# One gate pass and one value pass per expert, with the output blocks one by one between the next expert's input blocks

## The chip, the cores and the metric

The kernel runs on one core of one Trainium2 chip. The metric is the device time of one execution in microseconds. A core has a matrix engine (PE, with its weight loads on a row of its own, PEld), a vector engine (DVE), a scalar engine (ACT), a fourth compute engine (POOL) and a queue engine (SP) that issues nearly all transfers; 16 DMA engines carry those out.

## The reference, cut to what matters

Two layers over 256 tokens, in fp32. The first is Fourier and windowed attention with a dense SwiGLU, the second is differential attention with a SwiGLU of 8 experts, of which each token takes two. The change touches only the experts:

```python
def moe_swiglu(h, router_w, w_in, w_out):
    logits = jnp.einsum('btd,de->bte', h, router_w)
    top_vals, top_idx = lax.top_k(logits, TOP_K)             # TOP_K = 2
    gates = jax.nn.softmax(top_vals, axis=-1)
    ...
    for e in range(N_EXPERTS):                               # 8
        out = out + combine[..., e:e + 1] * swiglu(h, w_in[e], w_out[e])

def swiglu(h, w_in, w_out):                                  # 1024 -> 2 x 3584 -> 1024
    g, u = jnp.split(h @ w_in, 2, axis=-1)
    return (jax.nn.silu(g) * u) @ w_out
```

The weights of one expert are 1024 x 7168 and 3584 x 1024 numbers of 4 bytes, 44.04 MB; all eight are 352.3 MB.

## The kernel before

Each expert works on at most 96 gathered tokens (a "large" place) or 64 (a "small" one). The places 0, 2, 4, 6 are large, 1, 3, 5, 7 are small, and the last expert is so a small one. In words, for one expert: a gather (matrix products with a one-hot table) brings its tokens into PSUM, ACT writes them as `h_te` (L1047); the input passes multiply them with the gate and the value columns of `expert_in_w`; ACT takes silu of the gate sums (L1066), DVE multiplies by the value sums (L2290), PE turns the product round in 128x128 tiles (`transposes`, L1654), ACT copies the turned tiles to `work` (L1072); the output blocks multiply them with `expert_out_w` into PSUM; ACT and DVE split the result into two parts `y_split` (L1078, L2263), PE spreads it back to token order (`combine`, with `onehot_t`), and DVE adds it to `y_acc` (L2276).

The hidden width of 3584 is cut in two halves, A with 2048 columns and B with 1536. So an expert has four input passes (GA, UA, GB, UB) of 8 blocks each, one block for each 128 rows of the input: 128 partitions with rows of 8 KB (A) or 6 KB (B). Its output has 14 blocks of 256 rows, 1 MiB each, 8 for A and 6 for B. In all an expert has 46 blocks. The order in which PE uses them is one list, which also is the order of the transfers:

```python
LAST = in_pass("GB") + out_blocks("A", 0, 4) + in_pass("UB") + out_blocks("A", 4, 8)
CYCLE = LAST + in_pass("GA", 1) + out_blocks("B", 0, 3) + in_pass("UA", 1) + out_blocks("B", 3, 6)
LAST = LAST + out_blocks("B", 0, 6)
```

The passes GA and UA in a cycle are those of the next expert. The blocks land in 18 slots of 8 KB a partition, taken in turn (`RING0`); a B block fills three quarters of its slot. PE counts every block that it has used in the semaphore `used`, and SP fetches block n when block n - 18 has been used:

```python
sp.wait_ge(used, B_MOE + n - RING0 + 1)
fetch(0, min((n - len(HEAD)) // EB, NE - 1), n, order)
```

So SP's issues are in the order of use, and each slot is refilled as soon as PE is through with it. The first 18 blocks are fetched while the attention of the second layer still runs, as the places of its weights and buffers come free (the waits on `lo_done`, `scores`, `pv_done`, `used`, `hn_done` in SP's `experts`). Rounds 1 and 2 of `experts` serve tokens above the capacity, behind a branch on `overflow`; in the profiled execution they are not entered.

Of the kernel before, what the change touches and what calls it, by code (L numbers as in the profile page):

```python
# [41 lines left out]
HALVES = ("A", "B")  # L42
WIDTH = {"A": 2048, "B": 1536}
OUTS = {"A": 8, "B": 6}
ROUNDS = 3
RING0 = 18
RING = 14
# [22 lines left out]
def in_pass(what, ahead=0):  # L70
    return [("in", what, k, ahead) for k in range(DK)]


def out_blocks(half, m0, m1):
    return [("out", half, m, 0) for m in range(m0, m1)]


HEAD = in_pass("GA") + in_pass("UA")
LAST = in_pass("GB") + out_blocks("A", 0, 4) + in_pass("UB") + out_blocks("A", 4, 8)
CYCLE = LAST + in_pass("GA", 1) + out_blocks("B", 0, 3) + in_pass("UA", 1) + out_blocks("B", 3, 6)  # L80
LAST = LAST + out_blocks("B", 0, 6)
AFTER = {"GB": 8, "UB": 20, "GA": 32, "UA": 43}
EB = len(CYCLE)
ROUND = HEAD + CYCLE * (NE - 1) + LAST
assert len(ROUND) == NE * EB
assert GROUP * 3 == CAP
# [8 lines left out]
def act_columns(cap, half):  # L95

    return {CAP: 3, SMALL: 2}[cap] * WIDTH[half] // 4
# [7 lines left out]
PIECES = {CAP: [[(0, 96, 3, 0, 512, 0, 0)],  # L105
                [(96, 32, 3, 0, 512, 0, 512), (0, 32, 4, 0, 256, 32, 512), (32, 32, 4, 0, 256, 32, 768),
                 (64, 32, 4, 0, 256, 64, 512), (96, 32, 4, 0, 256, 64, 768)]],
          SMALL: [[(0, 64, 3, 0, 512, 0, 0)], [(64, 64, 3, 0, 512, 0, 512)]]}
# [57 lines left out]
def backbone(nc, x, c, ctx_in, c_ctx, ada_w, ada_b, norm_g, mix_in_w, mix_out_w, win_sink, diff_qkv_w,  # L166
# [9 lines left out]
    WRAW = sb("w_raw", [P, RAW, BLK])  # L176
# [54 lines left out]
    _, POST2 = area(("pad_p", [P, W0 - 4096], F32), ("post2", [P, 4, D], F32))


    (WMOE, HTE, YS, PTR, YACC, ONEHOT) = area(
        ("w_moe", [P, 2 * SPL, BLK], F32), ("h_te", [P, DK, CAP], F32), ("y_split", [P, 2, D], F32R),
        ("onehot_t", [P, 2 * P], F32R), ("y_acc", [P, XT, D], F32), ("onehot", [P, XT, CAP], F32))
    _, XW = area(("pad_x", [P, W0 - BLK], F32), ("w_extra", [P, BLK], F32))
    _, HN = area(("pad_b", [P, W0 + 12288], F32), ("h_nat", [P, XT, D], F32))
    TM = RES[:, 2, 0:400]
    SIL = RES[:, 2:4, :].rearrange("p a b -> p (a b)")[:, 512:2048]  # L240

# [47 lines left out]
    ACTT = work(10240, 2048)  # L289
    SPARE = work(6144, 2, BLK)  # L290
    FREED, QFREED = work(0, 2, BLK), work(4096, BLK)
# [19 lines left out]
    w_landed = [sem(f"w_landed{i}") for i in range(RING0)]  # L311
# [101 lines left out]
    hte_first = sem("hte_first")  # L413
# [14 lines left out]
    tr_ready = sem("tr_ready")  # L428
    actt_ready = sem("actt_ready")
# [6 lines left out]
    silu_half = sem("silu_half")  # L436
    act_half = sem("act_half")
# [61 lines left out]
    LATER = [0, 1] + list(range(5, 5 + RAW + 2 * SPL))  # L499
    early = (B_DOUT + 1) % SPL  # L500
    SPLIT_SLOTS = [early, SPL + early] + [j for j in range(2 * SPL) if j % SPL != early]
    assert len(LATER) == RING

    PLACE = [3, 4, 0, 1, 2] + list(range(5, RING0))

    def turn(n):

        i = (n - len(HEAD)) % EB
        return (i % RING, 4 if i < EB % RING else RING + EB % RING if i < RING else RING) if i < EB - EB % RING else \
            (i - EB + EB % RING, RING)  # L510

    def slot_of(rnd, n):
        return LATER[turn(n)[0]] if rnd else PLACE[n % RING0]

    def ring(r):

        if r < 5:
            return SPARE[:, r, :] if r < 2 else QFREED[:] if r == 2 else FREED[:, r - 3, :]
        if r < 5 + RAW:
            return WRAW[:, (N_RAW + r - 5) % RAW, :]  # L520
        return WMOE[:, SPLIT_SLOTS[r - 5 - RAW], :] if r < RING0 - 1 else XW[:]

    def moe_landed(rnd, e, n):

        slot = slot_of(rnd, n)
        if rnd == 0:
            return 16 * (n // RING0 + 1)
        first = 16 * sum(slot_of(0, m) == slot for m in range(len(ROUND)))
        fills = [m for m in range(len(ROUND)) if slot_of(rnd, m) == slot]
        each = 16 * sum(len(HEAD) <= m < len(HEAD) + EB for m in fills)  # L530
        return first + (rnd - 1) * 16 * len(fills) + e * each + 16 * sum(m <= n for m in fills)

    def moe_view(rnd, n):

        kind, what = ROUND[n][:2]
        w = ring(slot_of(rnd, n))
        return w.rearrange("p (j n) -> p j n", j=2) if kind == "out" else w[:, 0:WIDTH[what[1]]]

# [1869 lines left out]
```

## Time and profile before

| what | value |
|---|---|
| device time, median of 3 runs | 1671.93 us (1671.19 to 1673.8) |
| the profiled execution | 1671.87 us, of which the span is 1670.0 us |
| PE busy in the span | 95% |
| DVE, ACT busy | 31%, 23% |
| moved by DMA in the span | 474.42 MB, mean 284 GB/s |
| granted PE clock | 0.986 of full speed |

The span is what the trace shows; 1.87 us of the profiled execution's time lie outside it. The expert stage begins at about 828 us of the span and takes the second half. A busy PE is not a PE at its peak, since waits inside a run of matmuls count as busy when their records overlap.

### The profile page before, as it was taken

How to read it: one execution, taken by the hardware profiler on the slowest of the kernel's cores; microseconds unless marked ns; L12 is line 12 of the kernel's file. 1: busy time of each engine (PE TensorE's matmuls, PEld its weight loads, DVE VectorE, ACT ScalarE, POOL GpSimd, SP SyncE). 2: the span in 40 equal slices, each digit the busy share in tenths (PEclk: the TensorE clock that was granted, in tenths of full speed). 3: DMA queues.
4: the chain of work that ended last, by engine and by line, in shares of the span. 5: the costliest groups of instructions: out<-in, count | busy, mean ns of one | idle time of the engine just before them, and what ended most of it. 6: DMA issues, size and time to landing. Idle time of an engine off the chain costs nothing.

```text
span 1670.0 us, 28575 instructions
## 1 busy us (share of the span) xinstructions
PE 1583.0 (95%) x12596; PEld 953.8 (57%) x12596; DVE 519.8 (31%) x791; ACT 391.1 (23%) x655; POOL 34.5 (2%) x70
## 2 busy tenths in 40 slices
PE   5999989999999989998899999999999998999986
PEld 2855678878788877866536333463435533345232
DVE  3427467665533276357500010100101001010012
ACT  3327342221232243248400111000100001100011
POOL 1000100010000000000000000000000000000000
PEclk9999999999999999999899999999999999999998
DMA  9661816676523323213699999999999999999995
GB/s 368 210 226 36 258 51 202 199 256 231 217 85 120 117 82 126 101 51 138 253 318 390 417 418 421 417 419 418 418 421 418 419 418 418 420 418 419 418 418 213
DMA packets 106754, 474.42 MB, mean 284 GB/s; under 512 B 11176, under 2 KB 35144, under 8 KB 70784
## 3 DMA queue, kind: packets, MB, share of 16 engines
q1 hardware_dynamic: 103552, 467.64, 72.0%
q0 software_dynamic: 3072, 4.88, 1.1%
q8 instruction: 101, 1.65, 0.4%
q14 instruction: 29, 0.24, 0.0%
HBM read 471.36 MB, written 1.13 MB: 283 GB/s over the span
## 4 chain that ended last, share of the span: by engine, by line
PE 64%; SPq 19%; DMA 9%; DVE 5%; issue 2%; ACT 1%; DVEq 0%; ACTq 0%
PE ps L1140 62%; SPq L601 13%; SPq L598 6%; DMA w_moe<-in_expert_out_w_dram 2%; DMA work<-in_expert_out_w_dram 2%; DMA w_raw<-in_expert_out_w_dram 2%; DMA work<-in_expert_in_w_dram 1%; DMA w_raw<-in_ada_w_dram 1%; DMA w_moe<-in_expert_in_w_dram 1%; PE ps L1323 1%; DVE work L1835 1%; PE ps L1654 1%; DVE row_max L2103 1%; DVE w_lo L1766 0%; SPq L596 0%
## 5 line engine op out<-in xcount | busy, mean ns | idle before, releaser
L1140 PE MATMUL ps<-w_hi,h_t 128*128 128x512 f32 (+1 forms) x960 | 294.6, 388 | 11.5 <-DVE h_t L1824 5.4
L1140 PE MATMUL ps<-h_t,w_hi 128*128 128x512 f32 (+1 forms) x768 | 222.5, 374 | 6.2 <-DVE h_t L1824 6.2
L1140 PEld LDWEIGHTS ps<-w_hi,h_t 128*128 128x128 f32 x960 | 180.8, 191 | 49.0 <-issue 4.1
L1766 DVE TENSOR_TENSOR w_lo<-w_raw,w_hi 128x2048 fp32r<-128x2048 f32 x57 | 130.6, 2292 | 228.3 <-ACT w_hi L738 227.9
L1140 PE MATMUL ps<-w_lo,h_t 128*128 128x512 f32 (+1 forms) x480 | 185.4, 386 | 0.0
L2290 DVE TENSOR_TENSOR residual<-residual,ps 128x1152 f32<-128x1152 f32 (+3 forms) x15 | 19.4, 1292 | 529.1 <-PE ps L1140 529.1
L738 ACT ACTIVATE w_hi<-w_raw 128x2048 fp32r<-128x2048 f32 x57 | 108.9, 1913 | 301.7 <-PE ps L1140 301.4
L1140 PE MATMUL ps<-w_moe,h_te 128*32 128x512 f32 (+2 forms) x1830 | 170.6, 520 | 5.3 <-DMA w_moe<-in_expert_in_w_dram 4.4
L1140 PE MATMUL ps<-w_raw,h_te 128*32 128x512 f32 (+2 forms) x1694 | 159.5, 519 | 7.0 <-DMA w_raw<-in_expert_in_w_dram 6.1
L1140 PEld LDWEIGHTS ps<-h_t,w_hi 128*128 128x128 f32 x768 | 141.3, 191 | 33.8 <-issue 9.2
L1140 PE MATMUL ps<-work 128*32 128x512 f32 (+6 forms) x1104 | 141.9, 498 | 11.4 <-DMA work<-in_expert_out_w_dram 5.0
L1140 PE MATMUL ps<-work,h_te 128*32 128x512 f32 (+2 forms) x1662 | 147.4, 506 | 0.9 <-ACT h_te L1047 0.5
L1140 PE MATMUL ps<-h_t,w_lo 128*128 128x512 f32 (+1 forms) x384 | 143.4, 373 | 0.0
L1140 PEld LDWEIGHTS ps<-w_moe,h_te 128*32 128x32 f32 x1830 | 67.9, 110 | 102.6 <-issue 77.6
L1140 PEld LDWEIGHTS ps<-w_raw,h_te 128*32 128x32 f32 x1694 | 61.3, 110 | 98.9 <-issue 70.2
L1140 PEld LDWEIGHTS ps<-work,h_te 128*32 128x32 f32 x1662 | 65.6, 110 | 78.8 <-issue 61.7
L1140 PEld LDWEIGHTS ps<-w_lo,h_t 128*128 128x128 f32 x480 | 91.7, 191 | 17.6
L1140 PEld LDWEIGHTS ps<-work 128*32 128x32 f32 (+3 forms) x1104 | 53.4, 128 | 79.0 <-issue 52.2
L1140 PE MATMUL ps<-w_raw,work 128*32 128x512 f32 (+1 forms) x1024 | 93.8, 513 | 3.0 <-DMA w_raw<-in_expert_out_w_dram 3.0
L1140 PEld LDWEIGHTS ps<-h_t,w_lo 128*128 128x128 f32 x384 | 73.2, 191 | 12.5
L1140 PE MATMUL ps<-w_moe,work 128*32 128x512 f32 (+1 forms) x832 | 76.2, 515 | 1.6 <-DMA w_moe<-in_expert_out_w_dram 1.6
L1140 PEld LDWEIGHTS ps<-w_raw,work 128*32 128x32 f32 x1024 | 34.3, 110 | 58.7 <-issue 42.9
(274 smaller groups left out, 1210.2 us busy)
## 6 DMA issues: line engine op xcount, KB each, us to landing
w_raw<-in_ada_w_dram SPq DMA_DIRECT2D x48, 1024.0 KB, 5.3
w_raw<-in_expert_in_w_dram SPq DMA_DIRECT2D x43, 1024.0 KB, 24.7
w_moe<-in_expert_in_w_dram SPq DMA_DIRECT2D x42, 1024.0 KB, 26.1
w_raw<-in_expert_out_w_dram SPq DMA_DIRECT2D x40, 1024.0 KB, 23.7
work<-in_expert_in_w_dram SPq DMA_DIRECT2D x37, 1024.0 KB, 23.4
w_moe<-in_expert_in_w_dram SPq DMA_DIRECT2D x45, 768.0 KB, 22.0
work<-in_expert_out_w_dram SPq DMA_DIRECT2D x33, 1024.0 KB, 23.8
w_moe<-in_expert_out_w_dram SPq DMA_DIRECT2D x33, 1024.0 KB, 23.5
```

Of the source, the lines that this page charges most:

```text
L598: sp.dma_start(w, rows.rearrange("(p j) n -> p j n", j=2)).then_inc(done, 16)
L601: sp.dma_start(w, expert_in_w[0, e, b * P:(b + 1) * P, c0:c0 + WIDTH[what[1]]]).then_inc(done, 16)
L738: act.activation(WHI[:, b % SPL, :], WRAW[:, slot_w[b], :], ACT.Copy).then_inc(hi_done, 1)
L1140: return pe.matmul(out_, l, r, start=first, stop=last, skip_group_check=True)
L1323: ins = pe.transpose(ps[:, 4 + kv, c_ * P:(c_ + 1) * P], PR0[:, 2 * (u % 2) + kv, c_ * P:(c_ + 1) * P], ID[:])
L1654: ins = pe.transpose(ps[:, 5 + x // 4, P * (x % 4):P * (x % 4) + P], src, ID[:])
L1766: dve.tensor_tensor(WLO[:, b % SPL, :], WRAW[:, slot_w[b], :], WHI[:, b % SPL, :].bitcast(F32), ALU.subtract).then_inc(lo_done, 1)
L1835: ins = dve.tensor_scalar(TF[s][:, n % 2, 256 * k:256 * k + 256], ps[:, UNIT_BANK[s][st][u], 256 * k:256 * k + 256], ACOL[:, st, 2 * u + k ...
L2103: link(dve.tensor_reduce(MX[:, p:p + 2], ps[:, p ^ 2:(p ^ 2) + 2, :], AX_X, ALU.max))
L2290: dve.tensor_tensor(SIL[:, 0:n], SIL[:, 0:n], PSF[:, 0:n], ALU.mult).then_inc(act_done, 1)
```

## The change

The halves A and B are gone. An expert now has one gate pass G and one value pass U over all 3584 columns, 8 blocks each of 128 partitions with rows of 14 KB (1.75 MiB), and 14 output blocks of 1 MiB as before, in all 30 blocks. The sums of a pass fill five PSUM banks and a quarter of a sixth (three and a half for a small place; `BANKS`), and silu, product, transposes and the copies of the turned tiles go bank by bank (`silu_bank`, `prod_bank`, `tr_bank`, `actt_bank`). The output sums lie in banks 6 and 7. The output blocks of expert e stand one by one between the input blocks of expert e + 1, from its third gate block on; those of the last expert stand alone behind its transposes.

The slots are 8 of 14 KB for input blocks and 3 of 8 KB for output blocks. A freed slot takes the next block of its own kind; only when no input blocks are left do freed input slots (but one, `KEEP`) take output blocks. SP issues in the order in which slots are freed, which is no longer the order of use.

```diff
-HALVES = ("A", "B")
-WIDTH = {"A": 2048, "B": 1536}
-RING0 = 18
...
+EB = 2 * DK + ED // 256
+BANKS = {CAP: (512,) * 5 + (128,), SMALL: (512,) * 3 + (256,)}
...
+def first_round():
+    order = [("G", 0, k) for k in range(DK)] + [("U", 0, k) for k in range(DK)]
+    for e in range(NE - 1):
+        ins = [("G", e + 1, k) for k in range(DK)] + [("U", e + 1, k) for k in range(DK)]
+        for i, b in enumerate(ins):
+            order += [b] + ([("O", e, i - 2)] if i >= 2 else [])
+    return order + [("O", NE - 1, m) for m in range(ED // 256)]
+
+IN_SLOTS, OUT_SLOTS = 8, 3
+KEEP = 4
...
+    for n, b in enumerate(USES):
+        s = place[b]
+        if s < IN_SLOTS and ins:
+            nxt = ins.pop(0)
+        elif outs and s != KEEP:
+            nxt = outs.pop(0)
+        else:
+            continue
+        place[nxt] = s
+        fetches.append((nxt, n + 1))
...
-                for n in range(RING0, len(ROUND)):
...
-                    sp.wait_ge(used, B_MOE + n - RING0 + 1)
-                    fetch(0, min((n - len(HEAD)) // EB, NE - 1), n, order)
...
+                sp.wait_ge(lo_done, B_MOE - 4)
+                fetch(0, "G", 0, 0)
+                sp.wait_ge(lo_done, B_MOE - 2)
+                fetch(0, "G", 0, 1)
+                sp.wait_ge(scores, U0 + U1)
+                fetch(0, "G", 0, 2)
+                fetch(0, "O", 0, 0)
+                sp.wait_ge(pv_done, U0 + U1)
+                fetch(0, "G", 0, 4)
+                sp.wait_ge(lo_done, B_MOE)
+                fetch(0, "G", 0, 3)
+                sp.wait_ge(used, B_MOE)
+                for k in range(5, DK):
+                    fetch(0, "G", 0, k)
+                fetch(0, "O", 0, 1)
+                sp.wait_ge(hn_done, XT)
+                fetch(0, "O", 0, 2)
...
+                for (kind, e, i), after in FETCHES:
...
+                    sp.wait_ge(used, B_MOE + after)
+                    fetch(0, kind, e, i, order)
...
+            for b, n in enumerate(BANKS[cap]):
+                if first:
+                    hold(b)
+                for q in range(4):
...
+            for e in range(NE - 1):
+                transposes(e)
+                if e:
+                    pe.wait_ge(y_lo, 2 * e)
+                gather(e + 1)
+                product("G", e + 1, 0)
+                if e:
+                    pe.wait_ge(hte_ready, DK * (e + 2))
+                    combine(e - 1, 0, 6)
+                    combine(e - 1, 1, 7)
+                product("G", e + 1, 1)
...
+            e = NE - 1
+            transposes(e)
+            pe.wait_ge(y_lo, 2 * e)
+            for m in range(ED // 256):
+                product("O", e, m)
+                if m == 1:
+                    for i in range(4):
+                        combine(e - 1, i, i)
...
+            hte(0, CAP)
+            silu(0)
+            for e in range(NE):
+                if e:
+                    yhi(e - 1)
+                transposed(e)
+                turned(e)
+                if e == NE - 1:
+                    break
+                hte(e + 1, capacity(0, e + 1))
...
+                silu(e + 1)
```

In the diff `G`, `U` and `O` name a block's kind, and the expert and the block's number follow; its last two pieces are PE's and ACT's order. SP's first issues of the stage, before the change (a row with x5 stands for five transfers; 128x2048 are rows of 8 KB, 128x1536 of 6 KB):

```order
L601 DMA w_raw<-in_expert_in_w_dram 128x2048 x4
L601 DMA work<-in_expert_in_w_dram 128x2048 x5
L601 DMA w_raw<-in_expert_in_w_dram 128x2048 x2
L601 DMA w_moe<-in_expert_in_w_dram 128x2048 x5
L601 DMA w_moe<-in_expert_in_w_dram 128x1536
L601 DMA w_extra<-in_expert_in_w_dram 128x1536
L601 DMA work<-in_expert_in_w_dram 128x1536 x5
L601 DMA w_raw<-in_expert_in_w_dram 128x1536
L598 DMA w_raw<-in_expert_out_w_dram 128x2048 x4
```

and after it:

```order
L635 DMA w_moe<-in_expert_in_w_dram 128x3584 x2
L635 DMA work<-in_expert_in_w_dram 128x3584
L632 DMA work<-in_expert_out_w_dram 128x2048
L635 DMA work<-in_expert_in_w_dram 128x3584
L635 DMA w_moe<-in_expert_in_w_dram 128x3584 x4
L632 DMA w_moe<-in_expert_out_w_dram 128x2048
L632 DMA w_extra<-in_expert_out_w_dram 128x2048
L635 DMA w_moe<-in_expert_in_w_dram 128x3584 x2
```

The first fill was 16 blocks of 1 MiB and 2 of 0.75 MiB; it is now 8 of 1.75 MiB and 3 of 1 MiB.

PE at the end of the expert stage, before the change (`w_moe,h_te` is an input block, `w_..,work` or `work` alone an output block of 8 matmuls for a small place, L1654 transposes, `y_split` a combine, `mod_rows` the spread of the last gate):

```order
L1140 MATMUL ps<-w_moe,h_te 32x512 x4
L1140 MATMUL ps<-w_moe,h_te 32x256 x4
L1140 MATMUL ps<-w_moe,work 32x512 x8
L1140 MATMUL ps<-w_extra,work 32x512 x8
L1654 MATMUL ps<-ident,residual 128x128 x6
L1140 MATMUL ps<-work 32x512 x32
L1140 MATMUL ps<-mod_rows,ident 128x128 x8
L1140 MATMUL ps<-work 32x512 x8
L1140 MATMUL ps<-w_raw,work 32x512 x24
L1140 MATMUL ps<-y_split,onehot_t 128x512 x8
```

and after it:

```order
L1663 MATMUL ps<-ident,residual 128x128 x12
L1663 MATMUL ps<-ident,w_moe 128x128 x2
L1669 MATMUL ps<-ident,onehot 64x128 x2
L1170 MATMUL ps<-w_extra,work 32x512 x8
L1170 MATMUL ps<-w_moe,work 32x512 x8
L1170 MATMUL ps<-y_split,onehot_t 128x512 x8
L1170 MATMUL ps<-w_moe,work 32x512 x8
L1170 MATMUL ps<-work 32x512 x8
L1170 MATMUL ps<-mod_rows,ident 128x128 x8
L1170 MATMUL ps<-w_moe,work 32x512 x40
L1170 MATMUL ps<-work 32x512 x8
L1170 MATMUL ps<-w_extra,work 32x512 x8
```

Behind the last transposes stood 8 output blocks (32 + 8 + 24 matmuls, 8 to a block); now all 14 stand there, and with them the combine of the expert before.

PE at the boundary between the experts 1 and 2 (a small and a large place) after the change; `onehot,h_nat` is the gather:

```order
L1663 MATMUL ps<-ident,residual 128x128 x12
L1663 MATMUL ps<-ident,w_moe 128x128 x2
L1669 MATMUL ps<-ident,onehot 64x128 x2
L1170 MATMUL ps<-onehot,h_nat 128x96 x16
L1170 MATMUL ps<-w_moe,h_te 32x512 x20
L1170 MATMUL ps<-w_moe,h_te 32x128 x4
L1170 MATMUL ps<-y_split,onehot_t 128x512 x4
```

The transposes and the gather were apart before, each with blocks on both sides; they now stand together, with no block between them.

## Rows read from the trace of the kernel before

**Rows 1.** The page: span, DMA queue, chain's engines, one transfer kind (last: issue to landing).
```profile
span 1670.0 us, 28575 instructions
...
q1 hardware_dynamic: 103552, 467.64, 72.0%
...
PE 64%; SPq 19%; DMA 9%; DVE 5%; issue 2%; ACT 1%; DVEq 0%; ACTq 0%
...
w_raw<-in_ada_w_dram SPq DMA_DIRECT2D x48, 1024.0 KB, 5.3
```

**Rows 2.** Busy time by stretch; the last three columns are clock, DMA share, GB/s.
```profile
828.00:912.00 84.00, 81.75 (x950) 40.68 (x954) 4.79 (x10) 8.50 (x15) 0.00 (x0) 1.00 0.90 330
912.00:1640.00 728.00, 708.44 (x7582) 305.03 (x7578) 60.35 (x100) 66.25 (x122) 0.00 (x0) 1.00 1.01 418
1641.00:1652.00 11.00, 10.00 (x88) 3.99 (x92) 0.00 (x0) 1.08 (x2) 0.00 (x0) 1.00 0.55 226
```

**Rows 3.** The same view of two stretches with A blocks, then three with B blocks.
```profile
1000.00:1050.00 50.00, 50.00 (x482) 18.54 (x478) 0.95 (x1) 4.95 (x10) 0.00 (x0) 1.00 1.01 420
1200.00:1250.00 50.00, 49.41 (x466) 18.31 (x462) 0.95 (x1) 4.95 (x10) 0.00 (x0) 1.00 1.01 420
...
945.00:965.00 20.00, 20.00 (x216) 6.85 (x212) 0.00 (x0) 1.02 (x1) 0.00 (x0) 1.00 1.02 418
1145.00:1165.00 20.00, 20.00 (x216) 6.89 (x212) 0.00 (x0) 0.45 (x1) 0.00 (x0) 1.00 1.01 415
...
1270.00:1290.00 20.00, 19.95 (x267) 13.98 (x263) 4.18 (x7) 2.64 (x3) 0.00 (x0) 1.00 1.01 417
```

**Rows 4.** SP's issues in order of time: start, time until the last, line, transfer, count.
```profile
691.97 34.74 SPq L601 DMA_DIRECT2D w_raw<-in_expert_in_w_dram  x4
...
818.43 0.33 SPq L601 DMA_DIRECT2D w_extra<-in_expert_in_w_dram  x1
831.32 10.63 SPq L601 DMA_DIRECT2D work<-in_expert_in_w_dram  x5
```

**Rows 5.** PE in order of time; one matmul of the program is two records.
```profile
828.48 13.08 PE L1140 MATMUL ps<-work,h_te 128*32 128x512 f32 x120 [0.52 <-ACT h_te L1047]
...
875.91 1.70 PE L1654 MATMUL ps<-ident,residual 128*128 128x128 f32 x12
877.54 9.96 PE L1140 MATMUL ps<-work,h_te 128*32 128x512 f32 x150
...
894.89 5.37 PE L1140 MATMUL ps<-w_raw,work 128*32 128x512 f32 x64
...
982.03 2.11 PE L1140 MATMUL ps<-y_split,onehot_t 96*128 96x512 f32 x8
984.07 4.08 PE L1140 MATMUL ps<-w_moe,h_te 128*32 128x512 f32 x48
...
1005.74 3.81 PE L1140 MATMUL ps<-onehot,h_nat 128*128 128x96 f32 x32
...
1011.23 5.33 PE L1140 MATMUL ps<-w_moe,work 128*32 128x512 f32 x48
...
1027.73 10.48 PE L1140 MATMUL ps<-work,h_te 128*32 128x512 f32 x96
```

**Rows 6.** ACT and DVE in order of time, after one expert's outputs.
```profile
974.43 2.76 ACT L1078 ACTIVATE y_split<-ps 96x512 fp32r<-96x512 f32 x6 [28.19 <-PE ps L1140]
...
977.22 2.42 DVE L2263 TENSOR_TENSOR y_split<-ps,y_split 32x512 fp32r<-32x512 f32 x5 [1.48 <-ACT y_split L1078]
...
1009.59 2.69 ACT L1047 ACTIVATE h_te<-ps,mod_cols,scale_cols 128x96 f32<-128x96 f32 x8 [17.26 <-PE ps L1140]
```

**Rows 7.** The end: two rows of PE in order of time.
```profile
1645.78 2.05 PE L1140 MATMUL ps<-mod_rows,ident 8*128 8x128 f32 x16
...
1657.22 2.38 PE L1140 MATMUL ps<-y_split,onehot_t 64*128 64x512 f32 x8 [1.50 <-DVE y_split L2263]
```

**Rows 8.** The last transfer in the chain that ended last (start, length, what).
```profile
1627.61 26.15 DMA w_raw<-in_expert_out_w_dram
```

More of the change, by code:

```diff
@@ L512, in slot_of @@
[L512 to L525, printed above, removed]
-        if rnd == 0:
[L527 to L537, printed above, removed]
[L539 to L543 removed]
+    def slot_view_moe(s):
+        if s < IN_SLOTS:
+            at = (8192, 0, -4096, 4096, -1, 11776, 15360, 18944)[s]
+            if s == 2:
+                return work(4096, ED)
+            return work(0, ED) if s == KEEP else WMOE[:, at:at + ED]
+        return (work(7680, BLK), WMOE[:, 22528:24576], XW[:])[s - IN_SLOTS]
@@ L1053, in silu @@
-            def silu(e, half, after):
-                J = 2 * (NE * rnd + e)
-                act.wait_ge(used, after)
-                first = rnd == 0 and isinstance(e, int) and e == 0 and half == "A"
-                if not first:
-                    act.wait_ge(tr_ready, J + HALVES.index(half))
-                if first:
-                    for b in range(3):
-                        act.activation(SIL[:, 512 * b:512 * b + 512], ps[:, b, :],
-                                       ACT.Silu).then_inc(silu_half if b < 2 else silu_done, 1)
-                    return
-                n = act_columns(capacity(rnd, e), half)
-                act.activation(SIL[:, 0:n], PSF[:, 0:n], ACT.Silu).then_inc(silu_done, 1)
@@ L1114, in _ @@
+            for h in range(2):
+                act.activation(POST[3][0][:, 0, 512 * h:512 * h + 512], ps[:, 4 + h, :], ACT.Copy).then_inc(gate_kept, 1)
+            yhi(NE - 1)
         flag = []
@@ L1610, in out_block @@
+        def out_block(m, w):
+            for j in range(2):
+                first = m == 0 and j == 0
+                last = m == 13 and j == 1
+                for tg in range(3):
+                    mm(ps[group(tg), 6, :], hidden(m, j, tg), w[:, j, 0:512], first, last)
+                mm(ps[group(3), 6, :], hidden(m, j, 0), w[:, j, 512:1024], first, last)
                 for n, (tg, c_) in enumerate(QUARTERS):
-                    ins = mm(ps[group(n), 4, 0:256], hidden(half, m, j, tg),
+                    ins = mm(ps[group(n), 7, 0:256], hidden(m, j, tg),
@@ L2343, in experts @@
-            cycle(NE - 1, True)
-            gate(n0 + NE, order[NE - 1] + 1 if rnd == 0 else NE)
-            ylo(NE - 1)
-            for i in range(4):
-                accumulate(n0 + NE, i, i)
-            dve.wait_ge(acc_done, (n0 + 9) * 4 - 3)
+                with dve.Fori(0, NE) as e:
+                    onehot(place_of(e), e)
+                    product(e)
+                    ylo(e)
+                    gate(e, e)
+                    for i in range(4):
+                        accumulate(e, i, i)
@@ L2350, in _ @@
+            e = NE - 1
+            for x, bank in ((e - 1, 0), (e, 0)):
+                ylo(x)
+                gate(x, order[x])
+                for i in range(4):
+                    accumulate(x, i, i)
+            dve.wait_ge(acc_done, 4 * NE + 1)
         flag = []
```

685 lines of the change are left out of this document (318 added, 367 removed).

## The prediction

> **What bounds the kernel now.** I read the page first, then the stretches, then SP's and PE's order of time. The page says PE 64% and DMA 9% of the chain, SP's queue 19% [rows 1]; that looks like a PE kernel, but the expert stage has to be read by stretches. From 912 to 1640 us the 16 DMA engines are busy all the time (share 1.01) and move 418 GB/s [rows 2]. PE's busy time there is nearly full as well, but it works on blocks that the transfers let it have: what ends the stage is the last weight block, which lands at 1627.61 + 26.15 = 1653.8 us [rows 8], and after it come only one output block, the split, four combines and the finish. From 1641 to 1652 the share is only 0.55 at 226 GB/s [rows 2], with the last blocks still out: about half of the engines are through at 1641 and the others run to 1653. A block has landed when its slowest engine has delivered. So the pace that counts is not 418 but what lands: of 352.3 MB, 18.35 MB are the first fill (16 blocks of 1.049 MB, 2 of 0.786) and 84 x 0.330 = 27.7 MB come until 912 [rows 2, 4]; the other 306.2 MB take until 1653.8, 741.8 us, or 412.8 GB/s.
>
> Before 912 the transfers are not the bound. SP's first refill is at 831.32, after PE's first block from 828.48 on [rows 4, 5], and until 912 only 330 GB/s are moved [rows 2], since PE frees slots of 1 MiB that are refilled with 0.75 MiB blocks.
>
> **Step 1, the opening.** The first fill is 17 MiB in place of 17.5, and its places come free at the same events (691.97 to 818.43) [rows 4]. Large input blocks cost 13.08 / 5 = 2.62 (A) and 9.96 / 5 = 1.99 us (B) [rows 5]; the new block has the same matmul columns in both, 4.6 us. 16 of them: 828.5 + 73.6 = 902.1. Each frees 1.75 MiB and takes 1.75 MiB, 399 GB/s, so that at 902 all of 24 input and 3 output blocks are issued, 47.2 MB. Then PE frees nothing: 20 transposes at 1.70 / 12 = 0.14 us, 2 for the one-hot table, a gather of 3.81, and the first small input block, 10.48 / 6 + 4.08 / 3 = 3.1 us [rows 5]. The next slot is free at about 912.5, the next byte moves at 913.5, and the DMA engines stand idle for some 6 us. Yet at 913.5 47.2 MB are there, against 46.1 + 0.6 = 46.7 MB now: 1.2 us **gained**, no more.
>
> **Step 2, the rate of longer rows.** A block pair of 256 rows (8 and 6 KB) becomes one of 128 rows of 14 KB. Over the stage this takes 8 x 16 x 128 = 16384 of the 103552 packets away [rows 1]. Stretches in which only 8 KB rows move show 420 GB/s, stretches in which six tenths of the bytes come in 6 KB rows 418, 415 and 417 [rows 3]. With 16 engines that is 0.03810 and 0.03840 ns a byte for an engine; the difference over 0.6 x (1/6144 - 1/8192) gives 12.4 ns fixed cost a packet. An input block saves 8 packets an engine, 0.099 us; for the 104 input blocks after the opening 10.3 us **gained**. Bounds: nothing, if the differences in these rows are noise (the rows differ among themselves as much), and 15.6 us with 415 against 420. I take 10.3, the mean, for it rests on more than one row of each kind. The Trainium skill (DMA: Bandwidth & Descriptors, Why small descriptors are slow) puts the fixed cost of a packet at about 3 cycles and 32 bytes, and says that joining descriptors pays only at 256 bytes and below. By it the gain would be an estimated 4.7 ns a packet, 4 us in all, and the time some 6 us more than my sum.
>
> **Step 3, does PE keep up in the middle?** The same columns as before, so the blocks cost the same: large output 5.37 / 2, small output 5.33 / 3 [rows 5], with some 0.2 us of a run's last record taken off 2.65 and 1.74. New is that transposes and gather stand together behind the last output block of the expert before, whose sums have to leave banks 6 and 7 first: for a large one ACT's copies take 2.76 us [rows 6], DVE's subtractions end at 979.6, 2.4 us after ACT's 977.2 [rows 6], then come gather 3.81 and the first `h_te` (2.69 / 8) [rows 5, 6]: 9.5 us without a block, and 7.3 us where the transposes hide a small one's split. The combine costs 2.11 as before. A large input phase is 16 x 4.6 + 14 x 1.74 + 9.5 + 2.1 = 109.6 us, a small one 16 x 3.05 + 14 x 2.65 + 7.3 + 2.1 = 95.3; a pair 204.9. The transfers of a pair take 88.08 MB / 412.8 = 213.4, less 32 x 0.099 = 210.2. So PE keeps up, by 5 us a pair. Silu and product bank by bank cost nothing where PE's next bank covers them: ACT's six pieces of a split take 2.76 us [rows 6], some 0.5 us each, against 2.62 / 3 = 0.87 us of a bank on PE [rows 5]; without that cover it would be about 1 us an expert.
>
> But the order of issue matters. An output block is fetched when the one three before it has been used, behind the input blocks issued ahead, which are needed only eight input blocks later. PE thus waits for output blocks while its input blocks land some 30 us early, and the queue holds three pairs at most, 8.65 MB or 21 us (26 us now [rows 8]). Of these 2.8 us are latency (5.3 us from issue to landing without a queue [rows 1], of which 2.5 are the moving of 1 MiB) and 5.7 us PE's own pair; a gap of 9.5 us leaves some 3 us. I allow 0.6 us of idle DMA at three boundaries, 1.8 us **lost**.
>
> **Step 4, the end.** The last block for which PE waits is an output block of expert 6, about number 8, the last that is bound to three slots: from then on freed input slots take output blocks and these arrive faster than PE works. When it lands, 5 + 14 output blocks are still to come, 19.9 MB. PE then has, in one chain: 2.65 + 5 x (3.05 + 2.65) = 31.2; the boundary behind which expert 7's outputs start (split of expert 6 on ACT 2.76 [rows 6], then its copies of the turned tiles, four of about 0.5, and the start) 5.3; 14 x 1.74 = 24.4; combine 2.1, the gate's spread 2.05, the last split 1.5 and combine 2.4 [rows 5, 7]. Together 68.9 us. Now the same 19.9 MB from the end are due at 1653.8 - 48.3 = 1605.5, and PE's last record ends at 1657.22 + 2.38 = 1659.6 [rows 7], 54.1 us later, since PE follows the transfers. So the end **loses** 14.8 us: 6 more output blocks stand behind the last transposes, and the transfers are early for nothing.
>
> **The sum.** 352.3 - 47.2 - 19.9 = 285.2 MB at 412.8 is 690.9; less 10.3, plus 1.8, from 913.5 on: 1595.9. Plus 68.9 is 1664.8, plus 10.4 from PE's last record to the end of the span (1670.0 - 1659.6, unchanged) 1675.2, plus the 1.87 outside the span 1677.1. As differences: -1.2 - 10.3 + 1.8 + 14.8 = +5.1 on the profiled 1671.87, which is the median within 0.1. I forecast **1677 us**.
>
> **The rivals.**
> - *The rows bring little* (0.2): the difference in [rows 3] is noise. Then step 2 is worth nothing and the time is 1687, at half its worth 1682. For it: the rows scatter by 3 GB/s; against it: all three lie under both others. (The Trainium skill's rule named in step 2 is this case, at an estimated 1683.)
> - *The queue runs dry at the boundaries* (0.15): three output slots are too few. From the point at which a gap on PE with the latency is over the 3 us left, each microsecond more costs at seven boundaries 7 us; with 2 us 1691. For it: 26 us from issue to landing now, and landing goes by the slowest engine. The same time comes if PE's blocks of mixed banks cost over 2.5% more than now.
> - *The gain is larger than the end's loss* (0.2): faster. From step 2 alone at its upper bound the sum is -0.2 us, at 1671.7; a packet cost of 25 ns, which no row shows, or fast engines that no longer run 12 us ahead of the slow ones (226 GB/s at the end [rows 2]), whose evening out would be worth up to 1% of the transfers, gives 1664 to 1668.
> - *The forecast's own mechanism* (0.45): 1672 to 1681.
>
> **How the numbers follow.** A change within 0.2% (3.3 us) is about what a measurement cannot tell from none. Faster by more: the third rival, 0.18. Within: its rest and the lower part of my own case, where step 2 is at its upper bound, 0.2. Slower: the rest of my case and the first two, 0.62. The range runs from 1666 to 1690; it takes in both bounds of step 2 and part of the dry queue. My own case alone is 1672 to 1681.
>
> **What would show it.** DMA share about 1.0 from 914 on with 422 to 424 GB/s (step 2), a gap of some 6 us before 914 (step 1), PE's DMA waits nearly all on output blocks (step 3). At the end the last weights land at about 1645, well before PE needs them, and PE runs on without a DMA wait for 60 us or more (step 4). If PE still waits for the last output block, step 4 is wrong and the kernel is faster; if the share drops at each boundary, the second rival is right.

## The result and the profile after

The changed kernel takes 1690.61 us (median of 4 runs, 1687.96 to 1691.44) against 1672.87 (4 runs, 1671.19 to 1676.32) of the kernel before in the same measurement: a ratio of 1.0102, 95% interval 1.0090 to 1.0114. It is slower by 17.7 us. I had forecast slower, at 1677 us, with 1666 to 1690 as the range: the sign holds, the size is 13.6 us too small. The time lies 0.6 us above the range; as a change, 17.7 us lies just inside it (1690 is 18.1 us above the 1671.9 that the forecast started from). The rival of the dry queue stood at 1691.

From the page of the kernel after: span, PE, DMA share in 40 slices (tenths), GB/s in the same slices, the queue of the weights, and the issues of weight blocks with the median time from issue to landing in us.

```profile
span 1689.6 us, 27563 instructions
...
PE 1582.9 (94%) x12212; PEld 911.9 (54%) x12212; DVE 520.7 (31%) x810; ACT 394.4 (23%) x701; POOL 34.4 (2%) x70
...
DMA  9661816576524324114799999999999999899993
GB/s 367 205 225 51 254 35 213 189 271 227 198 100 136 101 74 132 69 44 163 296 404 375 424 423 368 424 424 424 424 366 424 424 423 424 355 424 424 423 379 126
...
q1 hardware_dynamic: 84096, 467.64, 70.5%
...
w_moe<-in_expert_in_w_dram SPq DMA_DIRECT2D x96, 1792.0 KB, 12.8
...
w_extra<-in_expert_out_w_dram SPq DMA_DIRECT2D x33, 1024.0 KB, 15.4
```

PE's busy time is that of before within 0.1 us:

```profile
PE 1583.0 (95%) x12596; PEld 953.8 (57%) x12596; DVE 519.8 (31%) x791; ACT 391.1 (23%) x655; POOL 34.5 (2%) x70
```

The same 467.64 MB were moved, in 19456 fewer packets (84096 in place of 103552, [rows 1]). The prediction counted 16384, those of the longer rows. By the sizes of the packets in both traces, 2048 more are packets of 4 bytes, one on each of 16 engines for each of the 128 transfers that are gone. The other 1024 come from a part of the change that the diff above doesn't show: before, two of the B output blocks of each large expert (`b in (3, 4)`) were fetched in rows of 4 KB, and now in rows of 8 KB like the rest. So nothing was added to the work; the time lies in gaps. The row of GB/s shows where: from the 23rd slice (930 us) on most stand at 423 or 424, above the 415 to 420 of before [rows 3], but three stand at 368, 366 and 355, and the last two at 379 and 126. Busy time by stretch, as in [rows 2] (the last three columns are clock, DMA share, GB/s):

```profile
828.00:912.00 84.00, 84.00 (x877) 32.65 (x879) 5.35 (x13) 11.39 (x26) 0.00 (x0) 1.00 0.89 354
912.00:1640.00 728.00, 687.77 (x7127) 263.48 (x7120) 54.81 (x104) 60.83 (x143) 0.00 (x0) 0.99 0.99 412
...
940.00:1000.00 60.00, 52.66 (x588) 18.16 (x584) 2.39 (x4) 2.07 (x4) 0.00 (x0) 1.00 1.01 424
1000.00:1020.00 20.00, 16.76 (x128) 10.97 (x124) 4.64 (x9) 7.57 (x19) 0.00 (x0) 0.83 0.93 374
1020.00:1040.00 20.00, 20.00 (x200) 6.69 (x196) 2.30 (x6) 0.00 (x0) 0.00 (x0) 1.00 0.93 361
1220.00:1240.00 20.00, 18.96 (x156) 10.14 (x160) 4.55 (x11) 3.44 (x11) 0.00 (x0) 0.91 0.86 336
1240.00:1260.00 20.00, 20.00 (x208) 6.39 (x204) 0.00 (x0) 0.00 (x0) 0.00 (x0) 1.00 0.97 390
...
1440.00:1460.00 20.00, 20.00 (x185) 8.39 (x188) 3.43 (x7) 2.04 (x7) 0.00 (x0) 0.97 0.80 296
1460.00:1480.00 20.00, 20.00 (x212) 6.32 (x204) 0.00 (x0) 0.00 (x0) 0.00 (x0) 1.00 0.98 403
```

What is missing from 424 GB/s in the six stretches of 20 us is 2.4 + 3.0, 4.2 + 1.6 and 6.0 + 1.0 us: 18.1 us of transfer time, at the three boundaries from a small to a large expert. The other boundaries show nothing of the kind (421 and 422 GB/s at 1100 to 1120 and 1320 to 1340).

PE at the first of these boundaries, in order of time (start, length, line, what, records, and in brackets the idle time before and what ended it):

```profile
1000.36 1.70 PE L1663 MATMUL ps<-ident,residual 128*128 128x128 f32 x12
...
1005.76 6.44 PE L1170 MATMUL ps<-onehot,h_nat 128*128 128x96 f32 x32 [3.24 <-DVE y_split L2286]
```

and SP's issues there:

```profile
996.79 0.33 SPq L635 DMA_DIRECT2D w_moe<-in_expert_in_w_dram  x1
1000.63 0.33 SPq L632 DMA_DIRECT2D w_moe<-in_expert_out_w_dram  x1
1017.06 6.11 SPq L635 DMA_DIRECT2D w_moe<-in_expert_in_w_dram  x2
```

For 16.4 us no block is ordered. That is 5.4 us of transposes and waiting for the split, the gather, and the first large input block, which must be through before its place is free. The gather takes 6.44 us where it took 3.81 [rows 5] (5.44 and 6.61 at the two other boundaries): after its 3.24 us of idleness PE works at a granted clock of 0.50, the lower of its two levels (1.2 in place of 2.4 GHz), as the stretches at this boundary show, the second of them up to 1011 us:

```profile
1002.00:1005.00 3.00, 0.52 (x5) 0.25 (x3) 1.68 (x4) 2.94 (x9) 0.00 (x0) 0.91 1.03 434
1005.00:1011.00 6.00, 5.24 (x25) 5.24 (x25) 0.87 (x3) 1.77 (x6) 0.00 (x0) 0.50 1.01 421
1011.00:1016.00 5.00, 5.00 (x45) 2.23 (x48) 0.00 (x0) 1.40 (x4) 0.00 (x0) 0.97 0.95 399
1016.00:1018.00 2.00, 2.00 (x24) 1.02 (x20) 0.38 (x1) 0.00 (x0) 0.00 (x0) 1.00 0.30 123
```

The DMA engines go on at full share until about 1013, then the share falls step by step, and from 1016 to 1018 their share is 0.30.

The end, PE in order of time:

```profile
1609.08 2.79 PE L1170 MATMUL ps<-w_extra,work 128*32 128x512 f32 x32 [1.00 <-DMA w_extra<-in_expert_out_w_dram]
...
1639.73 1.70 PE L1663 MATMUL ps<-ident,residual 128*128 128x128 f32 x12
...
1645.13 2.66 PE L1170 MATMUL ps<-w_extra,work 128*32 128x512 f32 x16 [3.24 <-DVE y_split L2286]
1647.55 2.92 PE L1170 MATMUL ps<-w_moe,work 128*32 128x512 f32 x16
...
1658.01 8.79 PE L1170 MATMUL ps<-w_moe,work 128*32 128x512 f32 x80
...
1676.90 2.29 PE L1170 MATMUL ps<-y_split,onehot_t 64*128 64x512 f32 x8 [1.52 <-DVE y_split L2286]
```

PE's last wait for a transfer ends at 1609.08; it is an output block of expert 6. From there to the last record, 1679.19, are 70.1 us without one, and the span ends 10.4 us behind that, as before.

### The profile page after: what moved, and what is told of

It is laid out like the page before. It is cut to its first block and busy times, and to the rows that moved or that the text cites. A ratio compares the mean times of both kernels' runs of the same rounds, so it can differ in the third digit from the quotient of the medians.

```text
span 1689.6 us, 27563 instructions
## 1 busy us (share of the span) xinstructions
PE 1582.9 (94%) x12212; PEld 911.9 (54%) x12212; DVE 520.7 (31%) x810; ACT 394.4 (23%) x701; POOL 34.4 (2%) x70
## 3 DMA queue, kind: packets, MB, share of 16 engines
q1 hardware_dynamic: 84096, 467.64, 70.5%
## 5 line engine op out<-in xcount | busy, mean ns | idle before, releaser
L1170 PE MATMUL ps<-w_moe,h_te 128*32 128x512 f32 (+2 forms) x3840 | 377.7, 540 | 0.0
L1170 PE MATMUL ps<-w_hi,h_t 128*128 128x512 f32 (+1 forms) x960 | 294.8, 388 | 11.5 <-DVE h_t L1846 5.4
L1170 PEld LDWEIGHTS ps<-w_moe,h_te 128*32 128x32 f32 x3840 | 122.1, 110 | 258.7 <-issue 251.1
L2311 DVE TENSOR_TENSOR residual<-residual,ps 128x512 f32<-128x512 f32 x24 | 16.5, 687 | 641.9 <-PE ps L1170 641.9
L1170 PE MATMUL ps<-work,h_te 128*32 128x512 f32 (+2 forms) x1280 | 126.5, 540 | 0.0
L1170 PE MATMUL ps<-w_moe,work 128*32 128x512 f32 (+1 forms) x972 | 99.3, 533 | 10.5 <-DMA w_moe<-in_expert_out_w_dram 10.5
L1113 ACT ACTIVATE y_split<-ps 32x256 fp32r<-32x256 f32 (+3 forms) x32 | 15.5, 483 | 394.0 <-PE ps L1170 393.6
L1170 PE MATMUL ps<-w_extra,work 128*32 128x512 f32 (+1 forms) x776 | 78.3, 527 | 14.3 <-DMA w_extra<-in_expert_out_w_dram 11.1
L1170 PEld LDWEIGHTS ps<-work,h_te 128*32 128x32 f32 x1280 | 41.3, 110 | 86.0 <-issue 83.8
L1094 ACT ACTIVATE residual<-ps 128x512 f32<-128x512 f32 x24 | 14.4, 598 | 303.6 <-PE ps L1170 303.6
L2055 DVE SCALAR_TENSOR_TENSOR work<-w_raw,cond_stationary,work 128x2048 f32<-128x2048 f32 x28 | 65.8, 2348 | 1.4
## 6 DMA issues: line engine op xcount, KB each, us to landing
w_moe<-in_expert_in_w_dram SPq DMA_DIRECT2D x96, 1792.0 KB, 12.8
work<-in_expert_in_w_dram SPq DMA_DIRECT2D x32, 1792.0 KB, 12.5
work<-in_expert_out_w_dram SPq DMA_DIRECT2D x36, 1024.0 KB, 14.5
w_extra<-in_expert_out_w_dram SPq DMA_DIRECT2D x33, 1024.0 KB, 15.4
```

The source lines that it names most:

```text
L1094: act.activation(sil(b, n), ps[:, b, 0:n], ACT.Silu).then_inc(silu_bank, upto(cap, b) - (upto(cap, b - 1) if b else 0))
L1113: ins = act.activation(YS[q0:q0 + np_, 0, d0:d0 + nc_], ps[p0:p0 + np_, bank, c0:c0 + nc_], ACT.Copy)
L1170: return pe.matmul(out_, l, r, start=first, stop=last, skip_group_check=True)
L2055: link(dve.scalar_tensor_tensor(out=total_, in0=w, scalar=c_, in1=total_, op0=ALU.mult, op1=ALU.add))
L2311: dve.tensor_tensor(sil(b, n), sil(b, n), ps[:, b, 0:n], ALU.mult).then_inc(prod_bank, upto(cap, b) - (upto(cap, b - 1) if b else 0))
```

## The experiments

All ran with the kernel before beside them on the same chip (medians 1673.1, 1673.5 and 1673.2 in the three measurements). The changed kernel's 1690.6 us is of an earlier measurement (1672.9 for the kernel before), so a difference to it, or between two of these measurements, is good to about 1 us. The theory that they test: the price comes from the order of issue that the separate places bring, at the three boundaries (too few output blocks on order) and at the end (PE's chain of 14 output blocks behind the last transposes), and the longer rows give part of it back. The rivals are named at each.

**Places: 6 and 6, 7 and 4, 6 and 3, 6 and 4.** The first two ran together.

```diff
-IN_SLOTS, OUT_SLOTS = 8, 3
+IN_SLOTS, OUT_SLOTS = 6, 6      # or 7, 4; 6, 3; 6, 4
...
-            at = (8192, 0, -4096, 4096, -1, 11776, 15360, 18944)[s]
+            at = (8192, 0, -4096, 4096, -1, 11776)[s]     # these lists as for 6 and 6
...
-        return (work(7680, BLK), WMOE[:, 22528:24576], XW[:])[s - IN_SLOTS]
+        return (work(7680, BLK), WMOE[:, 22528:24576], XW[:], WMOE[:, 15360:17408],
+                WMOE[:, 17408:19456], WMOE[:, 19456:21504])[s - IN_SLOTS]
...
-                for k in range(5, DK):
+                for k in range(5, IN_SLOTS):
                     fetch(0, "G", 0, k)
-                fetch(0, "O", 0, 1)
+                for m in (1, *range(3, OUT_SLOTS)):
+                    fetch(0, "O", 0, m)
```

> The changed kernel with 6 places for input blocks and 6 for output blocks (16.5 MiB) in place of 8 and 3 (17 MiB), so that blocks are issued in the order of use; nothing else differs. Theory (queue and end both come from the order of issue): no DMA idle at the three boundaries to a large expert (18 us less) and PE waits for output blocks until a few us before the end, so the end's 15 us shrink too: 1658 to 1665 us. Rival A (the end is lost anyhow, since 14 output blocks stand behind the last transposes): only the boundaries are cured, 1672 to 1676 us. Rival B (PE's gap at a boundary is what costs, whatever is queued): 1685 to 1691 us, the DMA share still falls at 1000, 1220 and 1440 us.

Measured: 1663.31 us (5 runs), ratio to before 0.9941 (0.9927 to 0.9954). That is 27.3 us under the changed kernel, and faster than the kernel before. The stretches that fell before, now:

```profile
940.00:1000.00 60.00, 56.75 (x626) 24.39 (x618) 5.62 (x11) 7.71 (x18) 0.00 (x0) 0.98 1.01 424
1000.00:1020.00 20.00, 20.00 (x188) 8.01 (x191) 3.71 (x8) 1.94 (x6) 0.00 (x0) 0.99 1.01 424
...
1220.00:1240.00 20.00, 20.00 (x208) 6.48 (x204) 0.00 (x0) 0.00 (x0) 0.00 (x0) 1.00 1.01 425
...
1440.00:1460.00 20.00, 20.00 (x208) 6.09 (x204) 0.00 (x0) 3.16 (x6) 0.00 (x0) 1.00 1.00 421
```

The boundary now begins at 990.73 us. PE waits as long for the split there, the clock falls and the gather takes 5.44 us. SP, too, orders nothing for 15.4 us:

```profile
996.14 5.44 PE L1172 MATMUL ps<-onehot,h_nat 128*128 128x96 f32 x32 [3.25 <-DVE y_split L2288]
```

```profile
991.00 0.33 SPq L633 DMA_DIRECT2D w_moe<-in_expert_out_w_dram  x1
1006.43 0.33 SPq L636 DMA_DIRECT2D work<-in_expert_in_w_dram  x1
```

Yet no fall is left, so rival B is out. PE now waits for input blocks as well, the last time for the last value block of expert 7, and its chain from there to the end is 46.3 us in place of 70.1 (1604.79 to 1651.08, the end of the last row):

```profile
1604.79 3.21 PE L1172 MATMUL ps<-w_moe,h_te 128*32 128x512 f32 x32 [1.00 <-DMA w_moe<-in_expert_in_w_dram]
...
1615.92 3.64 PE L1172 MATMUL ps<-work 128*32 128x512 f32 x16 [3.25 <-DVE y_split L2288]
...
1648.80 2.28 PE L1172 MATMUL ps<-y_split,onehot_t 64*128 64x512 f32 x8 [1.52 <-DVE y_split L2288]
```

So the 14 blocks behind the last transposes don't cost 15 us by themselves (rival A is out too). How long PE's chain behind its last wait is depends on the places, and with them on the order of delivery.

> The changed kernel with 7 places for input blocks and 4 for output blocks. Theory (order of issue): the queue holds one output block more, the boundaries lose at most 1 us of DMA each and the last DMA wait of PE comes some 5 us earlier from the end than with 8 and 3: 1667 to 1675 us. Rival A (the end is lost anyhow): 1673 to 1677. Rival B (PE's gap itself costs): 1685 to 1691 us.

Measured: 1675.16 us (11 runs), ratio 1.0011 (1.0001 to 1.0020). The boundaries stand at 426, 400 and 395 GB/s where they stood at 374, 336 and 296, and PE's last DMA wait ends at 1601.20, 58.9 us before its last record. The time lies 0.2 us above the theory's window, which is within the noise, and in rival A's; only the run with 6 and 6 tells those apart.

> The changed kernel with 6 places for input blocks and its 3 for output blocks (13.5 MiB in place of 17). Theory (the three output places alone decide: PE waits for output blocks while input blocks lie ready some 30 us early): two input places less cost next to nothing, 1689 to 1694 us, with the same falls of the DMA share at three boundaries. Rival (the bytes that are on order in all decide, since a gap of PE uses them up): 3.5 MiB less on order are 8 us of transfers less in the queue, every boundary loses several us more, 1700 us or more.

Measured: 1692.37 us (4 runs), 1.8 above the changed kernel. The first boundary reads 385 and 364 GB/s in its two stretches (374 and 361 with 8 and 3). Two input places less, 3.5 MiB, cost next to nothing. The same time comes about in another way, though. PE's last DMA wait ends here:

```profile
1620.04 2.79 PE L1171 MATMUL ps<-w_moe,work 128*32 128x512 f32 x32 [1.00 <-DMA w_moe<-in_expert_out_w_dram]
```

That is 11.0 us later than in the changed kernel, and the chain behind it, to 1678.94, is 58.9 us, 11.2 shorter. So the length of this chain is no loss by itself.

> The same with 6 and 4 places (14.5 MiB, 2.5 MiB less than the changed kernel has). Theory (the number of output places decides): no fall at the boundaries to speak of, and the last DMA wait of PE later, 1668 to 1676 us, so no worse than 7 and 4 (1675). Rival (the bytes on order decide): slower than the changed kernel, 1691 us or more.

Measured: 1673.35 us (11 runs), ratio 1.0000 (0.9991 to 1.0009). One output place of 1 MiB more than in the run before is worth 19.0 us, and with 14.5 MiB this kernel is 17 us faster than the changed one with 17. The bytes on order in all don't decide, the output places do. PE's last DMA wait here:

```profile
1609.92 2.79 PE L1171 MATMUL ps<-w_moe,work 128*32 128x512 f32 x32 [1.00 <-DMA w_moe<-in_expert_out_w_dram]
...
1659.27 2.36 PE L1171 MATMUL ps<-y_split,onehot_t 64*128 64x512 f32 x8 [1.52 <-DVE y_split L2287]
```

Its chain from there to the end is 51.7 us, against 58.9 with 6 and 3. The page's slices at the boundaries read at least 401 GB/s, against 355 to 386 there.

**The clock.** PE is given work in the gap.

```diff
                 transposes(e)
                 if e:
+                    if e % 2:
+                        for _ in range(20):
+                            pe.transpose(ps[:, 4, 0:128], ID[:], ID[:])
                     pe.wait_ge(y_lo, 2 * e)
```

and the same 20 ahead of the last expert's output blocks.

> The changed kernel, with 20 more transposes of the identity into an unused bank ahead of PE's wait for the split at the three boundaries and before the last expert's output blocks (2.8 us of PE work, which change no result), so that PE isn't idle for 3.24 us there. Theory (the granted clock falls to 1.2 GHz because PE idles, and this takes 2.6 us from the queue at each of three boundaries and about 1.2 us at the end): gather at 3.7 us in place of 6.44, DMA idle 9 to 11 us in place of 18, 1680 to 1684 us. Rival (the clock falls for another reason, or the slots alone decide): gather stays at 6.4 us or the time stays within 2 us of 1690.6.

Measured: 1684.69 us (5 runs), 5.9 under the changed kernel, 0.7 us above the window. PE and its clock at the first boundary:

```profile
1007.01 3.81 PE L1170 MATMUL ps<-onehot,h_nat 128*128 128x96 f32 x32 [1.07 <-DVE y_split L2291]
```

```profile
1005.00:1011.00 6.00, 4.93 (x45) 4.51 (x47) 2.07 (x6) 3.15 (x10) 0.00 (x0) 1.00 1.00 417
```

The gather is back at 3.81 us and the clock at 1.00, and the gather takes 3.81 us at the two other boundaries too. So the idle PE was the cause of the lower level. The stretches read 412, 365, 339, 389, 337 and 413 GB/s, which by the same sum as above leaves 13.6 us missing in place of 18.1, where I expected 9 to 11. So 4.5 us of the boundaries' price are the clock. The two traces agree: PE's last DMA wait ends at 1605.02, 4.1 us earlier, and its chain from there is 68.4 us, 1.7 us shorter than 70.1. The rest of the dry queue stays.

**The rows.** Each input block comes in two transfers.

```diff
-                sp.dma_start(w, expert_in_w[0, place, i * P:(i + 1) * P, c0:c0 + ED]).then_inc(done, 16)
+                for a, z in ((0, 2048), (2048, ED)):
+                    sp.dma_start(w[:, a:z], expert_in_w[0, place, i * P:(i + 1) * P, c0 + a:c0 + z]).then_inc(done, 16)
```

The counts that PE waits for are raised with it.

> The changed kernel, with each input block fetched by two transfers of 8 KB and 6 KB rows into the same place: the same bytes at the same events, 8 more packets an engine and input block. Theory (12.4 ns fixed cost a packet, which was step 2's gain): 0.1 us a block, of which what lies in the 110 input blocks' transfers comes back as time, 1698 to 1702 us, and 418 GB/s between the boundaries in place of 424. Rival (rows bring nothing): within 2 us of 1690.6 and still 424 GB/s.

Measured: 1696.95 us (4 runs), 6.3 above the changed kernel, 1.1 under the window, far from the rival. The stretch without a boundary falls from 424 to 418 GB/s as expected:

```profile
940.00:1000.00 60.00, 51.64 (x578) 17.66 (x573) 2.39 (x4) 2.07 (x4) 0.00 (x0) 1.00 1.01 418
```

Its stretches at the boundaries miss 16.4 us of 418 GB/s, against 18.1 of 424: slower transfers seem to be partly made good where the queue would run dry. So the same edit was made where it doesn't:

> The kernel with 6 and 6 places, with each input block fetched by two transfers of 8 KB and 6 KB rows (same bytes, 8 more packets an engine and block). Here the transfers bind without a gap from 912 to 1605 us. Theory (12.4 ns fixed cost a packet): 104 blocks x 0.099 = 10.3 us, 1672 to 1675 us. Rival A (only the 6.3 us that the same edit cost the changed kernel): 1668 to 1671. Rival B (rows bring nothing): within 2 us of 1663.3.

Measured: 1670.77 us (11 runs), 7.5 above 6 and 6. That lies at the upper end of rival A's window and 1.2 us under the theory's, though it is more than the 6.3 us of the run before. The rate over the long stretch, of this kernel and then of 6 and 6:

```profile
912.00:1604.00 692.00, 669.57 (x6983) 262.77 (x6979) 52.48 (x100) 60.76 (x142) 0.00 (x0) 0.99 1.01 418
```

```profile
912.00:1604.00 692.00, 675.78 (x7057) 263.33 (x7049) 52.45 (x100) 60.75 (x142) 0.00 (x0) 0.99 1.01 423
```

423 against 418 is 8.3 us of the 692; the time shows 7.5. Divided by 104 blocks and 8 packets, 7.5 to 8.3 us are 9 to 10 ns a packet. The cost is real, and 20 to 27% smaller than the 12.4 ns taken from [rows 3].

A rival remains: the edit doubles the input transfers as well as the packets, and the cost could lie with a transfer. No run separates them, but the single packets of these two traces do in part. From 912 to 1600 us a packet of 8 KB takes 315 and one of 6 KB 238 ns (mean), one of 14 KB 541 ns, so that the pair takes 12 ns more. That is some 95 ns for a block and engine, while the second transfer brings each engine one packet of 4 bytes, which takes 9 ns. So nearly all of it lies with the packets. By these times 104 blocks would cost 10.8 us; why the device time shows 7.5 is open.

**The end.** The same half of the last expert's work is left out after and before the change.

```diff
-            for j in range(2):
+            for j in js:                      # (0,), for the last block (1,), in the last expert
```

> The changed kernel, in which each output block of the last expert is used for half of its rows: half of the matmuls of these 14 blocks are left out (its result is not the reference's), all transfers stay. Theory (step 4: the end is PE's chain, the transfers are early for nothing): 14 x 0.87 = 12.2 us less, 1678 to 1681 us. Rival (the last blocks' transfers or their order bind the end): 1686 to 1691 us.

Measured: 1679.06 us (8 runs), 11.5 less, within the theory's window.

> The kernel before, with the same half of the matmuls of the last expert's 14 output blocks left out (its result is not the reference's). Theory (before, PE follows the transfers to the end, only the last block's own work stands behind them): 0 to 2 us less, 1670.5 to 1673 us. Rival (PE's chain binds before too, so that the end costs the change nothing): 6 to 12 us less.

Measured: 1673.55 us (11 runs), ratio 0.9998 (0.9989 to 1.0007): no gain, and 0.6 us above the window, since the kernel before took 1673.5 us here and not 1672.9. PE stands there before nearly every block, waiting for its transfer:

```profile
1643.15 1.06 PE L1140 MATMUL ps<-work 128*32 128x512 f32 x8 [1.43 <-DMA work<-in_expert_out_w_dram]
...
1652.83 3.96 PE L1140 MATMUL ps<-w_raw,work 128*32 128x512 f32 x24
```

The second row is a caution: the last three half blocks take 3.96 us, where 24 such records at full clock take 2.7 (4.50 for 40 in the half kernel after the change). PE had idled ahead of nearly every block, and its granted clock stood at 0.50 from 1646 to 1655 us, which hides 1.3 us of them, and some in the rows ahead. The pair says that half of the work is worth 11.5 us after the change and little before it, and that is step 4's claim; it doesn't say exactly nothing.

**The gap at the end.** In the kernel with 6 and 6, PE is idle for 3.25 us behind the last transposes, and its next two blocks take 3.64 + 3.04 us in place of 1.9 each.

```diff
             transposes(e)
-            pe.wait_ge(y_lo, 2 * e)
             for m in range(ED // 256):
                 product("O", e, m)               # sums in bank 4, not 6, for this expert
-                if m == 1:
+                if m == 3:
+                    pe.wait_ge(y_lo, 2 * e)
                     for i in range(4):
                         combine(e - 1, i, i)
...
-                if e:
+                if 0 < e < NE - 1:
                     yhi(e - 1)
                 transposed(e)
                 turned(e)
+                if e == NE - 1:
+                    yhi(e - 1)
```

> The kernel with 6 and 6 places, in which the last expert's output blocks are summed in bank 4 in place of bank 6, so that they needn't wait for the split of expert 6; ACT copies the turned tiles ahead of that split, the combines of expert 6 and the spread of the gate come two blocks later (and the spread uses banks 5 and 7). Theory (the 3.25 us in which PE is idle there, and the half clock after it, stand in PE's chain to the end): 2.4 us less idle and 3 us less at 1.2 GHz, 1657 to 1659 us. Rival (the last transfers, which end at 1640 us, or the split put off hold the end): 1661 to 1664 us.

Measured: 1662.22 us (5 runs), ratio 0.9931 (0.9918 to 0.9945), 1.1 under 6 and 6, which the intervals can't tell from none: the rival's window. The gap is gone (0.53 us), but PE waits for the last four blocks instead:

```profile
1637.96 1.92 PE L1181 MATMUL ps<-w_moe,work 128*32 128x512 f32 x16 [1.24 <-DMA w_moe<-in_expert_out_w_dram]
...
1645.40 1.92 PE L1181 MATMUL ps<-w_moe,work 128*32 128x512 f32 x16 [0.55 <-DMA w_moe<-in_expert_out_w_dram]
```

```profile
1633.00:1645.00 12.00, 9.49 (x84) 2.16 (x76) 0.00 (x0) 0.00 (x0) 0.00 (x0) 1.00 0.44 180
```

I had taken 1640 us as the end of the transfers from the share in the stretches, which is a mean of 16 engines. The last block lands at 1645, at a mean share of 0.44 over the last 12 us. With 6 and 6 PE's chain and the transfers end almost together, and this kernel waits for its last blocks as the kernel before does. It is 28.4 us under the changed kernel and 11.3 under the kernel before.

## Why the prediction was wrong in size, step by step

**Step 1, the opening: held.** From 828 to 912 us 354 GB/s were moved, 29.7 MB, with the first fill of 17.8 MB 47.5 MB; I had 47.2. The engines' share from 908 us on, in stretches of 2 us, is 0.20, 0.66 and 0.72, then 1.04: some 3 us of idleness in place of 6. No run isolates the 1.2 us of this step.

**Step 2, the rate: right in kind, a little too large.** 10.3 us were taken off; the split rows cost 6.3 us in the changed kernel and 7.5 where no gap takes it back. The rival that rows bring little is refuted by both.

The way to the 12.4 ns was partly luck. The three lower stretches of [rows 3] are not "six tenths of the bytes in 6 KB rows": by the sizes of their packets these carry 75, 30 and 56% of the bytes, and the 4 KB rows named above, which I had overlooked, 2, 25 and 0%. The lowest rate, 415 GB/s, is that with the most of them. With the extra packets counted as they are, the three give some 11 ns together. The 1024 packets that the 4 KB rows cost are an estimated 0.6 us of the change's gain, at 9 to 10 ns each on 16 engines; no run has them alone.

The rule that I weighed there (the Trainium skill, DMA: Bandwidth & Descriptors, Why small descriptors are slow), by which I had estimated 4.7 ns a packet, is not borne out at these sizes: the runs give about twice that.

**Step 3, idle DMA at the boundaries: this is the term that failed.** It was 1.8 us, and the trace has 18.1. The sentence that fails is "the queue holds three pairs at most, 8.65 MB or 21 us". Three output places are three pairs only if PE uses none of them. But PE stands waiting for an output block, and when it lands, that block's own place is still taken; the orders still out are two pairs, 5.77 MB or 13.7 us at 422 GB/s. The page agrees: 12.5 to 12.8 us from issue to landing for an input block, 14.0 to 15.4 for an output block. Against that stand 16.4 us without an issue, where I had 9.5 + 5.7 = 15.2; the lower clock, which I hadn't foreseen, is 2.6 of them. A queue of 13.7 us doesn't cover 16.4 and the start of a transfer, nor 13.8 without the clock's part, as the run with PE kept busy shows; one of 21 would have. With 13.7 in place of 21 the prediction's own count gives 15.2 + 2.8 - 13.7 = 4.3 us at each boundary, 13 us at three; that run misses 13.6. The fourth place adds a pair, 6.8 us, and so mends it, which 6 and 3 against 6 and 4 show (1692.4 and 1673.4 us), both with fewer bytes on order than the changed kernel. Of the rival "the queue runs dry at the boundaries" the mechanism was right, and its time by luck: it had 2 us at seven boundaries, and there are some 6 us at three. Into a small expert the gather takes 3.68 us at full clock, and PE doesn't wait for the split.

**Step 4, the end: the count held, its reason did not.** The last block for which PE waits is an output block of expert 6, as written, and from it PE's chain is 70.1 us for 68.9. The lower clock behind the 3.24 us of waiting is 1.8 us of it (1645.13 and 1647.55: 2.66 and 2.92 us in place of 1.9 each), and with PE kept busy the chain is 68.4 us. Half of the work there is worth 11.5 us, 12.2 were expected, and close to nothing before the change. What I had wrong is the reason behind it: "6 more output blocks stand behind the last transposes". They do in the kernel with 6 and 6 as well, and there the end costs less, since the transfers are in the order of use and still under way. The last weights came at about 1663 us, not at 1645 (share 0.81 at 1661, 0.16 at 1662). On the way the engines ran nearly dry once more, with a share of 0.02 to 0.38 from 1646 to 1649; this cost nothing, as PE has no DMA wait there.

**The sum.** PE's last DMA wait ends at 1609.1, forecast 1595.9. To these 13.2 us the idle time adds 16.3 and the rows 2.0 to 4.0, which is 5 to 7 us too much. I think that it is the lag of the slowest engine: the pace of 412.8 GB/s by which I counted had it priced in, and in a gap the slow engines catch up while the fast ones stand (the share falls over some 5 us and not at once). That was argued, not tested. By the runs, the change splits without it: from 6 and 6 to the changed kernel 27.3 us for the places and the order of issue that they bring; from 6 and 6 to the kernel before 9.8 us the other way, of which the rows are 7.5.

## What to carry to other kernels

With separate places for two kinds of blocks, count the orders that are out at the moment when the consumer waits: places less the one in use, of the kind it waits for, and compare that with the longest time in which it frees none, its first block after the gap included. Places of the other kind don't help, and orders in the sequence of use do with less memory. A gap of 3.24 us on PE cost more than itself here: the gather behind it ran in part at half clock and took 1.6 to 2.8 us more.

## What the runs showed of the hardware

- After 3.24 us of idleness PE's granted clock went to 0.50, at the first boundary for some 6 us (gathers of 6.44, 5.44 and 6.61 in place of 3.81 us); with 2.35 us of transposes put into that time, and 1.07 us of idleness left, it stayed at 1.00.
- Rows of 14 KB, with the 8 KB rows of the outputs, move at 423 to 424 GB/s where 8 and 6 KB rows move at 418: 9 to 10 ns of time for each packet saved. A packet of 14 KB takes 541 ns, those of 8 and 6 KB together 553.
- The 16 DMA engines don't finish together: their mean share was 0.44 over the last 12 us before the last block landed. A stretch's share says when the mean is done, not when the last block is there; I misread it in the expectation of the last kernel.
